# Three weight chunks of expert pair 14 loaded ahead into other buffers; result loads and output stores issued by SyncE

## The reference

```
N_EXPERTS = 32; TOP_K = 2; D_MODEL = 1024; D_EXPERT = 512
tok = h.reshape(T, D)
g_sel = argmax(tok @ w_group + b_group)                  # one of 4 groups
top_l, top_i = top_k(e_logits[g_sel], TOP_K)             # 2 of its 8 experts
weight = p_group * softmax(top_l)
...
def expert_block(e, rows):                               # rows: the tokens of expert e
    a = xb @ w_gate[e]; u = xb @ w_up[e]                 # 1024 -> 512
    return (silu(a) * u) @ w_down[e]                     # 512 -> 1024
out = sum over the two experts of a token, weighted
return rmsnorm(x + out, final_g)
```

## Time and profile before

| | us |
|---|---|
| time, median of 3 runs (lowest, highest) | 1720.37 (1717.6, 1721.54) |
| the profiled execution, its own time | 1719.1 |
| its span (first to last instruction) | 1717.2 |
| PE busy | 1491.0 |
| DVE busy | 585.8 |
| POOL busy | 496.5 |
| ACT busy | 475.3 |
| transfers in the span | 317.30 MB, 185 GB/s on average |
| share of the chain that ended last: PE / DMA / DVE | 64% / 19% / 10% |

### The profile page before, as it was taken

One profiled execution on the slowest core, in us unless ns is written; L12 is line 12 of the kernel. 1 busy time (PEld: TensorE's weight loads), 2 busy tenths in 40 slices (PEclk: granted clock), 3 DMA queues, 4 the chain that ended last, 5 costly groups with the idle time before them and its releaser, 6 DMA issues.

```text
span 1717.2 us, 18601 instructions
## 1 busy us (share of the span) xinstructions
PE 1491.0 (87%) x7132; PEld 979.2 (57%) x7133; DVE 585.8 (34%) x964; ACT 475.3 (28%) x818; POOL 496.5 (29%) x298
## 2 busy tenths in 40 slices
PE   7999999999699999999996998995877778778781
PEld 5975667887588888788674674574322322223220
DVE  3146553232633333312507695745000000000003
ACT  4245564222433333311334324221000000000001
POOL 3431134444344444444233364322010100100001
PEclk9999999999899999999997999996999999998996
DMA  7323002332223333233232221065999999999973
GB/s 283 108 87 85 1 2 65 95 99 88 83 88 97 99 87 97 86 98 96 77 98 80 74 86 61 25 245 180 400 427 426 427 428 426 426 424 424 422 335 154
DMA packets 47974, 317.30 MB, mean 185 GB/s; under 512 B 7664, under 2 KB 7664, under 8 KB 35360
## 3 DMA queue, kind: packets, MB, share of 16 engines
q1 hardware_dynamic: 38224, 288.84, 44.1%
q0 software_dynamic: 9104, 25.41, 4.0%
q10 hardware_dynamic: 576, 2.10, 0.3%
HBM read 307.99 MB, written 14.68 MB: 188 GB/s over the span
## 4 chain that ended last, share of the span: by engine, by line
PE 64%; DMA 19%; DVE 10%; issue 3%; ACT 2%; POOL 1%; SPq 0%; POOLq 0%; ACTq 0%; DVEq 0%
PE banks L357 24%; DMA arena<-experts 18%; PE banks L387 11%; PE banks L945 8%; PE banks L1924 3%; PE banks L840 2%; PE banks L367 2%; PE banks L1853 2%; PE banks L1869 1%; PE banks L697 1%; PE banks L1836 1%; PE banks L698 1%; PE banks L1840 1%; DVE arena_r L1701 1%; PE banks L967 1%
## 5 line engine op out<-in xcount | busy, mean ns | idle before, releaser
L335 POOL TENSOR_TENSOR arena_r<-ring,arena_r 128x1024 fp32r<-128x1024 f32 x143 | 356.9, 2497 | 510.8 <-ACT arena_r L320 510.8
L357 PE MATMUL banks<-hT_r,arena_r 128*128 128x512 f32 x1216 | 399.1, 398 | 8.5 <-DVE arena_r L1701 5.7
L945 PE MATMUL banks<-ring,arena 128*64 128x512 f32 x768 | 242.2, 620 | 65.3 <-DMA arena<-experts 45.3
L320 ACT ACTIVATE arena_r<-ring 128x1024 fp32r<-128x1024 f32 x143 | 151.2, 1059 | 525.6 <-PE banks L357 325.3
L357 PE MATMUL banks<-arena_r 128*128 128x512 f32 x800 | 294.0, 392 | 0.0
L357 PEld LDWEIGHTS banks<-hT_r,arena_r 128*128 128x128 f32 x1216 | 228.6, 188 | 72.4 <-issue 8.9
L945 PEld LDWEIGHTS banks<-ring,arena 128*64 128x64 f32 x768 | 79.9, 142 | 215.4 <-issue 157.8
L387 PE MATMUL banks<-arena_r 128*128 128x512 f32 x784 | 188.2, 394 | 3.7 <-POOL arena_r L335 3.7
L357 PEld LDWEIGHTS banks<-arena_r 128*128 128x128 f32 x800 | 150.2, 188 | 34.6
L387 PEld LDWEIGHTS banks<-arena_r 128*128 128x128 f32 x784 | 146.9, 188 | 39.6 <-POOL arena_r L335 5.4
L596 POOL DMA_INDIRECT back<-arena,at_out x16 | 16.2, 1014 | 441.2 <-DVE arena L1442 224.3
(11 more groups left out here) (419 smaller groups left out, 1809.4 us busy)
## 6 DMA issues: line engine op xcount, KB each, us to landing
arena<-experts SPq DMA_DIRECT2D x48, 2048.0 KB, 21.6
ring<-experts SPq DMA_DIRECT2D x48, 2048.0 KB, 18.2
ring<-stream SPq DMA_DIRECT2D x163, 512.0 KB, 3.5
rows<-arena POOLq DMA_DIRECT2D x8, 512.0 KB, 6.4
arena<-back POOLq DMA_DIRECT2D x8, 512.0 KB, 6.8
grow<-grows POOLq DMA_DIRECT2D x5, 512.0 KB, 4.5
resid<-x ACTq DMA_DIRECT2D x4, 512.0 KB, 5.3
out<-arena POOLq DMA_DIRECT2D x4, 512.0 KB, 3.1
```

Of the source, the lines that this page charges most:

```text
L320: nc.scalar.activation(parts(name, m)[:, 0, :], tile(tile_n), ACT.Copy).then_inc(S["w_high"], 1)
L335: nc.gpsimd.tensor_tensor(w[:, 1, :], tile(tile_n), plain(w[:, 0, :]), ALU.subtract).then_inc(S["w_low"], 1)
L357: last = nc.tensor.matmul(pb[:, bank, :], w[:, a, k * P:(k + 1) * P], b[:, k, :], start=(k == 0 and part == 0), stop=(k == ND - 1 and part ...
L945: last = nc.tensor.matmul(pb[r, bank, :], XT[:, k, r], chunk(c + e)[:, k * 512:(k + 1) * 512], start=(k == 0), stop=(k == ND - 1))
```

## The change

Four things change.

1. Chunks 0, 1 and 2 of pair 14 (`SPARE[0]` is 14) get places of their own. Chunk 0 goes to `hT`, chunk 1 to the first 4096 columns of `arena`, where the normalised tokens lay, and chunk 2 in three pieces to two parts of `arena` around the routing's numbers and to `junk`. SP issues them right behind pair 0's chunks: the first when the router's matmuls are done, the second when the stores to `rows` have landed, the third when `counts_out` has been raised.
2. SP's loop over pairs ends at pair 13. Pairs 14 and 15 are written out: pair 14 loads chunks 3, 4, 5 only, and pair 15's chunks 0 to 2 wait for pair 13's products, not for pair 14's. PE's loop ends at pair 13 too, and its pairs 14 and 15 are written out; pair 14 reads chunks 0 to 2 from the new places.
3. The eight loads of `back` and the four output stores are issued by SP. POOL raises `fin_go` when the scatters have landed, and SP waits for it.
4. DVE's copy of the counts moves behind five small operations (the softmax of the routing weights), since those read numbers where a piece of chunk 2 will lie.

```
+        SPARE = (N_PAIR - 2, [[(hT[:, :, :].rearrange("p k t -> p (k t)"), 0, CHUNK)], [(ar(0, CHUNK), 0, CHUNK)],
+                              [(ar(4096, 1536), 0, 1536), (ar(6656, 1536), 1536, 3072), (junk[:, :], 3072, CHUNK)]])
...
         def second_pool(pool):
...
-            for i in range(NT):
-                for c in range(2):
-                    pool.dma_start(G[:, 2 * i + c, :], back[(NT * c + i) * P:(NT * c + i + 1) * P, :]).then_inc(S[f"back{i}"], 16)
-            for i in range(NT):
-                pool.wait_ge(S["fin_y"], i + 1)
-                pool.dma_start(out[i * P:(i + 1) * P, :], xo[:, i, :]).then_inc(S["out_st"], 16)
-            pool.wait_ge(S["out_st"], 16 * NT)
+            pool.sem_inc(S["fin_go"], 1)
...
         def expert_stream(sp):
...
+            def spare_in(c):
+                for place, first, end in SPARE[1][c]:
+                    sp.dma_start(place, EX[6 * SPARE[0] + c, :, first:end]).then_inc(S["spare_in"], 16)
+
+            sp.wait_ge(S["w_used"], W_EXP)
+            spare_in(0)
+            sp.wait_ge(S["rows_st"], 16 * 2 * NT)
+            spare_in(1)
+            sp.wait_ge(S["counts_out"], 1)
+            spare_in(2)
+
-            with sp.Fori(1, N_PAIR) as b:
+            with sp.Fori(1, SPARE[0]) as b:
                 for c in range(6):
                     sp.wait_ge(done[c // 2], b)
                     sp.dma_start(chunk(c), EX[b * 6 + c, :, :]).then_inc(chunk_in[c], 16)
+            for b in range(SPARE[0], N_PAIR):
+                for c in range(3 if b == SPARE[0] else 0, 6):
+                    sp.wait_ge(done[c // 2], b - 1 if c < 3 and b > SPARE[0] else b)
+                    sp.dma_start(chunk(c), EX[b * 6 + c, :, :]).then_inc(chunk_in[c], 16)
...
+            sp.wait_ge(S["fin_go"], 1)
+            for i in range(NT):
+                for c in range(2):
+                    sp.dma_start(G[:, 2 * i + c, :], back[(NT * c + i) * P:(NT * c + i + 1) * P, :]).then_inc(S[f"back{i}"], 16)
+            for i in range(NT):
+                sp.wait_ge(S["fin_y"], i + 1)
+                sp.dma_start(out[i * P:(i + 1) * P, :], xo[:, i, :]).then_inc(S["out_st"], 16)
+            sp.wait_ge(S["out_st"], 16 * NT)
...
         def second_pe(pe):
...
-            with pe.Fori(0, N_PAIR // 2) as turn:
+            with pe.Fori(0, SPARE[0] // 2) as turn:
                 for q in range(2):
                     pair_pe(turn * 2 + q, turn, q)
+            for q in range(2):
+                pair_pe(SPARE[0] + q, SPARE[0] // 2, q, q > 0)
```

More of the change, by code:

```diff
@@ L138 @@
 xg_in0 xg_in1 idx_in
-at_in at_out gathers scatters y_st0 y_st1 back0 back1 back2 back3 moe_x fin_y""".split()
+spare_in fin_go at_in at_out gathers scatters y_st0 y_st1 back0 back1 back2 back3 moe_x fin_y""".split()
 NORMS = ["n1", "n2", "n3", "n4", "n5"]
@@ L472, in chunk, with spare @@
             return ar(8192 + CHUNK * (c - 3), CHUNK)
+        SPARE = (N_PAIR - 2, [[(hT[:, :, :].rearrange("p k t -> p (k t)"), 0, CHUNK)], [(ar(0, CHUNK), 0, CHUNK)],
+                              [(ar(4096, 1536), 0, 1536), (ar(6656, 1536), 1536, 3072), (junk[:, :], 3072, CHUNK)]])
+        def spare(c, a, b):
+            for place, first, end in SPARE[1][c]:
+                if first <= a and b <= end:
+                    return place[:, a - first:b - first]
         fbias, rsum_b = grow[:, 0:512], grow[:, 512:1024]
@@ L932, in turn_rows, with both_in, weights, product @@
                     last.then_inc(S["x_tr"], 1)
[L934 to L941, removed]
+            def both_in(b, c, skipped):
+                for v in (c, c + 1):
+                    if isinstance(b, int) and b == SPARE[0] and v < 3:
+                        pe.wait_ge(S["spare_in"], 16 * sum(len(places) for places in SPARE[1]))
+                        continue
+                    left = 1 if v < 3 and skipped else 0
+                    pe.wait_ge(chunk_in[v], b * 16 + 16 * ((landings(4 * v) if v < 3 else 0) + 1 - left))
+            def weights(b, c, first, end):
+                return spare(c, first, end) if isinstance(b, int) and b == SPARE[0] and c < 3 else chunk(c)[:, first:end]
+            def product(b, c, bank, done, skipped):
+                both_in(b, c, skipped)
                 for k in range(ND):
@@ L944, in product @@
                         r = slice(e * ROWS, (e + 1) * ROWS)
-                        last = nc.tensor.matmul(pb[r, bank, :], XT[:, k, r], chunk(c + e)[:, k * 512:(k + 1) * 512],
+                        last = nc.tensor.matmul(pb[r, bank, :], XT[:, k, r], weights(b, c + e, k * 512, (k + 1) * 512),
                                                 start=(k == 0), stop=(k == ND - 1))
@@ L954, in turn_hidden, with down @@
                 last.then_inc(S["h_tr"], 1)
-            def down(b):
+            def down(b, skipped):
                 pe.wait_ge(S["h_ev"], b + 1)
@@ L961, in down @@
                 pe.wait_ge(S["y_ev_dve"], b + 1)
-                both_in(b, 4)
+                both_in(b, 4, skipped)
                 for h in range(2):
@@ L969, in down, with pair_pe @@
                 last.then_inc(S["ex_down"], 1)
-            def pair_pe(b, half, q):
+            def pair_pe(b, half, q, skipped=False):
                 turn_rows(b, half, q)
@@ L975, in pair_pe @@
                 pe.wait_ge(S["x_ev_act"], b + 2)
-                product(b, 0, 0, S["ex_gate"])
-                product(b, 2, 1, S["ex_up"])
+                product(b, 0, 0, S["ex_gate"], skipped)
+                product(b, 2, 1, S["ex_up"], skipped)
                 turn_hidden(b)
-                down(b)
+                down(b, skipped)
             pe.wait_ge(S["counts_out"], 1)
-            with pe.Fori(0, N_PAIR // 2) as turn:
+            with pe.Fori(0, SPARE[0] // 2) as turn:
                 for q in range(2):
                     pair_pe(turn * 2 + q, turn, q)
+            for q in range(2):
+                pair_pe(SPARE[0] + q, SPARE[0] // 2, q, q > 0)
             pe.wait_ge(S["over_ready"], 1)
@@ L992, in second_pe @@
                         with pe.If(valid > 0):
-                            pair_pe(turn * 2 + (N_PAIR + q), turn + N_PAIR // 2, q)
+                            pair_pe(turn * 2 + (N_PAIR + q), turn + N_PAIR // 2, q, True)
         def second_act(act):
@@ L1428, in second_dve @@
             L(TT(RT[:, 884:888], RT[:, 880:884], RT[:, 308:312], ALU.mult))
+            counts = RT[0:1, 1400:1432]
+            nc.vector.tensor_copy(counts, pb[0:1, 0, 0:32]).then_inc(S["counts_out"], 1)
             def pair_rows(b, half, q):
```

4 lines of the change are left out of this document (1 added, 3 removed).

## The result

The changed kernel takes 1699.85 us (median of 4 runs, 1698.01 to 1701.17), the kernel before 1719.24 in the same comparison; the ratio is 0.9886, with a 95% interval of 0.9868 to 0.9903. That is 19.4 us less. I had forecast 4 us less, and a range that ended at 1709.5. The profiled execution has a span of 1697.2 us against 1717.2, so its 20.0 us can be laid out stage by stage.

What follows compares the result with a forecast made beforehand. The prediction took the expert stage to be bound by its DMA transfers. Its terms, -10.5 + 7.2 - 0.8 = -4.1 us, took the median from 1720.4 to 1716.3 us, with a range of 1709.5 to 1721.5.

Steps and rivals of the forecast that it cites:

- Term 3: End of the kernel: SP issues result loads and output stores faster than POOL; 0.8 us less, between 0 and 2.
- Term 2: Head, before gate product 0: the early chunks delay gather 0, 7.2 us more, between 0 and 14.
- (a): Head: gather 0 is issued 0.9 us late, as the first early chunk slows the stores to rows.
- (b): Head: gather 0 lands 6.3 us slower beside the early chunks, as scatters under load do; between 0 and 10.0.
- rival B: Head: queues take turns packet for packet, gather 0 costs 3.5 us instead of 7.2, median 1712.6; chance 0.23.
- Term 1: Tail, from up product 13: three chunks fewer to transfer, PE bounds the last two pairs; 10.5 us less.
- The dry queue: Tail: SP's queue runs dry some 3 us while pair 14's chunk 4 waits for down 13; 0.5 us taken off.
- Rival D: Tail: after the dry queue pair 15's chunks come 5 us late and PE waits; median 1721.3; chance 0.12.
- The costs at nothing: Moved counts copy (1 us if uncovered), SP's five new issues (1.7 us of SP) and written-out pairs add no time.

Runs made afterwards that it cites:

- two_after_gather: The changed kernel, but the second and third early chunks are issued only after gathers 0 and 1 have landed: 1694.31 us, ratio 0.9859 to the kernel before.
- all_after_gather: The changed kernel, but all three early chunks are issued only after gathers 0 and 1 have landed: 1697.01 us, ratio 0.9876 to the kernel before.
- spares_only: The kernel before with only the early chunks, pairs 14 and 15 written out and the moved counts copy: 1716.29 against 1717.82 us, ratio 0.9992.
- the last experiment: The changed kernel with the second and third early chunks after gathers 0 and 1, and SP's last nine chunks reordered: 1696.06 us, ratio 0.9872.
- shift_192: The kernel before with an unused tensor of 192 bytes a partition ahead of grow: 1709.06 against 1717.25 us, ratio 0.9953.

## Why the prediction was wrong

**The step that failed first is one that isn't in it.** The sum has three terms for three parts; the fourth part of the diff, the twelve columns, was neither costed nor named as a rival. It is worth 9.3 us by itself; no other term misses by as much. No row of the trace before could have priced it, since all of its operations ran at one place of the arena. But it could have been named, with a bound to either side as a wider range. What the runs showed in its place: the arena's start on a multiple of 128 bytes, and products of the up stage that start every 226 ns instead of 233. With the columns alone added the measured time would still lie just under the range (1699.85 + 9.3 = 1709.2); it takes the next term as well.

**Term 3 was mis-sized, -0.8 where it is -6.4 (measured alone), outside its bound of 0 to 2.** SP's 0.33 us an issue holds for the output stores; its result loads took 0.43 (median). The issue is worth about what I said even so: from the last down product's end to DVE's first sum 10.9 us became 10.3. What failed is that the term ended with the last store. That store was issued at 1708.04 in a span of 1717.2, and I didn't ask what the 9.2 us behind it were. They held 3.3 us to the landing and a drain of 5.5.

**Term 2 was right in sum, by two errors that cancel.** Forecast +7.2, measured +7.9. (a) The gather's issue was 3.7 us late, not 0.9: from the router's end it came after 21.3 us instead of 17.6. The last store to `rows` took 20.4 us to land instead of 15.4, so nearly the whole first early chunk went ahead of it; the upper bound, 4.1, was the better value. (b) The landing was 4.2 us longer, not 6.3 (8.77 against 4.56 us). That lies between the row of the loaded scatters (6.3) and rival B's turn-taking (2.6). Both parts together are 7.9 us, where rival B had 3.5. The plain packet-for-packet reading of the Trainium skill's page "DMA: Bandwidth & Descriptors", section "Queues, rings and completion order", is too cheap here as well, by a factor of 1.6, if a packet of the profile is taken for one of that page's, which no run here shows. That these are the two parts of the delay, and both avoidable, two_after_gather and all_after_gather show.

**Term 1 was right in sum, by two smaller errors that cancel.** Forecast -10.5, measured -10.4 in the changed kernel and in spares_only. PE bounds the last two pairs: of the 14.7 us of transfer that are taken out, 4.3 stay unused. The dry queue costs 1.5 us, where I had taken off 0.5: PE waits 0.9 for pair 15's chunk 3, and 1.3 for its chunk 5 where it would have stood 0.7 for ScalarE in any case. The pieces of the sum were 0.9 us too long (67.9 us without these waits, not 68.8: 13.97 us for a pair's gate and up products instead of 14.2, and 10.9 to 11.0 between pairs instead of 11.2). I had written that the prediction is wrong if PE waits in pair 15. By that sign it was wrong here too, though the waits are of about a microsecond. Issuing pair 15's chunks into the gap brings no gain, which the last experiment showed. Rival D, with a wait of 5 us, did not come about.

**The costs at nothing.** The moved copy of the counts cost nothing: the five operations ahead of it take 1.0 us, it is done at 1176.1, and PE waits for gather 0 until 1188.1. The new loop and the written-out pairs left no trace up to up product 13: from gate product 0 it takes 406.6 us before and 406.7 after.

Terms 1 and 2 together, forecast at -3.3 us, are -2.5 in the changed kernel's trace and -1.4 in that of spares_only (-10.4 + 9.0), whose median is 1.5 us lower. The other 16 us of the gain are the columns (9.3 measured alone) and the drain (6.4).

## What to carry to other kernels

Read every line of a diff as an edit, those that only change a table's width too: what lies behind it in memory moves, and here 64 bytes were worth about as much as the three edits that had a purpose. Follow the chain to the end of the span, not to the last instruction that works; what stands between is someone's landing or drain, and an engine with a long drain should finish issuing early. And "the DMA engines are idle here" holds only until the stretch's small, urgent transfers are counted: bulk loads into a gap belong behind the transfer that the restart waits for.

## What was not expected of the hardware

In the up stage the same fp32r product of 512 columns started every 226 to 228 ns with its operands in an arena at a multiple of 128 bytes, and every 231 to 234 ns at 64 or 96 beyond one (840 and 832 products in 190 us at full clock, against 812 to 824). From 290 to 380 us the changed kernel had 389 where the kernel before had 393, and shift_192 had 396, so each stretch has its own best place. All told it is 0.5 to 0.6% of this kernel. The page "SBUF — State Buffer" of the Trainium skill, section "Operand start alignment", says that its measurements there are about legality and not speed; here the start has a speed. By which path it acts (the weight loads or the moving operand) no run here tells apart; instructions of the other engines beside the products are not needed for it.

A drain on GpSimd took 4.6 us when its last transfer was a scatter that had landed, 5.5 behind the output stores, and 13.0 when it began with its loads still being issued, against 13 ns on SyncE after the same four stores.
